# Column projections of the second stack's even layer as three rounded products, with the bias table loaded one phase later

## The reference, cut to what matters

```python
def even_mixer(hx, hc, w_in, gate_b, conv_w, conv_b, rpb, ml_norm_g, w_out, ctx_out):
    naq_x, nak_x, nav_x, mlqk_x, mlv_x, mlo_x, mlg_x = jnp.split(hx @ w_in, list(EVEN_SPLITS), axis=-1)
    naq_c, nak_c, nav_c, mlqk_c, mlv_c, mlo_c, mlg_c = jnp.split(hc @ w_in, list(EVEN_SPLITS), axis=-1)
    ...
    na_x = neighbourhood_attention(heads(naq_x), heads(nak_x), heads(nav_x),
                                   heads(nak_c), heads(nav_c), rpb)
    q_x, k_x, v_x, if_x, lf_x, ib_x, lb_x = _mlstm_inputs(mlqk_x, mlv_x, mlg_x + gate_b, conv_w, conv_b)
```

## Time and profile before

| | us |
|---|---|
| median of 3 runs | 3216.32 |
| lowest and highest of them | 3211.57, 3219.78 |
| the profiled execution | 3223.3 |
| its span in the trace | 3221.5 |
| TensorE busy | 2937.8 (91%) |
| VectorE busy | 1856.9 (58%) |
| ScalarE busy | 1409.2 (44%) |
| column projections, first to last product | 111.8 |

### The profile page before, as it was taken

How to read it: one execution, slowest core, us unless ns; L and a number is a source line. 1 busy time by engine, 2 the same in 40 slices (tenths; PEclk the granted TensorE clock), 3 DMA queues, 4 the chain that set the end, 5 groups by cost and what they waited for, 6 DMA issues and landing times. The chain is left out here.

```text
span 3221.5 us, 38728 instructions
## 1 busy us (share of the span) xinstructions
PE 2937.8 (91%) x15533; PEld 2270.3 (70%) x15533; DVE 1856.9 (58%) x2272; ACT 1409.2 (44%) x1799; POOL 13.5 (0%) x13
## 2 busy tenths in 40 slices
PE   6999899988799999999999989999779989799797
PEld 4799689777576676766766764448668767657796
DVE  3555454425688888888888830224444543345675
ACT  3221244324466676666666731223233333343554
POOL 0000000000000000000000000000000000000000
PEclk9999799999799999999999989899689999899898
DMA  4400364643799999989989973110012222201352
GB/s 158 144 1 1 138 228 171 262 144 132 275 361 345 351 342 346 347 339 345 350 334 352 359 277 94 62 53 4 14 61 92 92 92 79 78 35 40 120 182 79
DMA packets 94030, 585.86 MB, mean 182 GB/s; under 512 B 20400, under 2 KB 21504, under 8 KB 24480
## 3 DMA queue, kind: packets, MB, share of 16 engines
q1 hardware_dynamic: 91888, 580.26, 48.5%
q10 hardware_dynamic: 1968, 3.14, 0.3%
HBM read 582.31 MB, written 1.05 MB: 181 GB/s over the span
## 5 line engine op out<-in xcount | busy, mean ns | idle before, releaser
L2000 DVE TENSOR_TENSOR s_w_low<-weight_ring,s_w_high 128x2048 fp32r<-128x2048 f32 x336 | 759.7, 2289 | 127.0 <-ACT s_w_high L1939 123.2
L1939 ACT ACTIVATE s_w_high<-weight_ring 128x2048 fp32r<-128x2048 f32 x336 | 630.0, 1909 | 130.3 <-PE bank L1920 107.7
L254 DVE TENSOR_TENSOR s_w_low<-weight_ring,s_w_high 128x1024 fp32r<-128x1024 f32 x238 | 289.3, 1221 | 195.4 <-ACT s_w_high L239 195.2
L239 ACT ACTIVATE s_w_high<-weight_ring 128x1024 fp32r<-128x1024 f32 x238 | 249.5, 1051 | 282.9 <-PE bank L502 282.9
L502 PE MATMUL bank<-s_x_high,s_w_low 128*128 128x256 f32 (+1 forms) x1056 | 341.0, 323 | 28.9 <-DVE s_w_low L254 28.9
L1920 PE MATMUL bank<-s_w_high,s_x_low 128*96 128x512 f32 x896 | 356.4, 398 | 7.6 <-DVE s_w_low L2000 7.6
L1920 PE MATMUL bank<-s_w_high,s_x_high 128*96 128x512 f32 x896 | 356.8, 398 | 0.0
L1920 PE MATMUL bank<-s_w_low,s_x_high 128*96 128x512 f32 x896 | 354.4, 396 | 0.0
L502 PE MATMUL bank<-s_x_low,s_w_high 128*128 128x256 f32 (+1 forms) x1056 | 339.4, 321 | 0.0
L502 PE MATMUL bank<-s_x_high,s_w_high 128*128 128x256 f32 (+1 forms) x1056 | 339.2, 321 | 0.0
L356 PE MATMUL bank<-s_w_high,s_x_low 128*128 128x512 f32 x544 | 220.5, 405 | 59.8 <-DVE s_w_low L254 59.8
(11 more groups left out here) (468 smaller groups left out, 4164.8 us busy)
## 6 DMA issues: line engine op xcount, KB each, us to landing
weight_ring<-moe_w SPq DMA_DIRECT2D x336, 1024.0 KB, 6.7
weight_ring<-ada_w SPq DMA_DIRECT2D x48, 1024.0 KB, 6.1
weight_ring<-ffn_up SPq DMA_DIRECT2D x44, 1024.0 KB, 4.8
weight_ring<-ffn_w_in SPq DMA_DIRECT2D x22, 1024.0 KB, 4.9
weight_ring<-ffn_down SPq DMA_DIRECT2D x22, 1024.0 KB, 4.8
weight_ring<-ffn_w_down SPq DMA_DIRECT2D x11, 1024.0 KB, 4.8
weight_ring<-w_rkv_cols SPq DMA_DIRECT2D x8, 1024.0 KB, 8.3
weight_ring<-moba_qk SPq DMA_DIRECT2D x8, 1024.0 KB, 9.7
```

The lines of the kernel that those rows point to most:

```text
L239: K.nc.scalar.activation(self.hi[:, b, :], self.source(c, i), ACT.Copy).then_inc(*self.high.up())
L254: K.nc.vector.tensor_tensor(self.lo[:, b, :], self.source(c, i), self.hi[:, b, :], ALU.subtract)\
L1939: nc.scalar.activation(halves(whi, kind, n, i), raw(kind, n, i), ACT.Copy).then_inc(S["high"].h, 1)
L2000: V.tensor_tensor(halves(wlo, kind, n, i), raw(kind, n, i), halves(whi, kind, n, i), ALU.subtract)\
```

## The change

The function `linear_cols` is replaced, for this layer alone, by a new one, `split_cols`. It makes the parts of the 512 tokens once (ACT copies, DVE subtracts, four pieces of 128 x 1024 each), splits the weights by `Split` with depth 1, and issues three `fp32r` products where one in 32-bit floats stood: 384 of 128 x 128 by 128 x 512. The order of the outputs, the banks and the copies out are as before. The parts lie over units that nothing has filled yet: `x_high` over units 0 and 1, `w_high` over 2, `w_low` over 4, `x_low` over 7 and 8. Since `bias` is units 1 and 2, its 32 loads and that of `window` move from the column to the row projections, and the addition of `window` moves on DVE from the beginning of that phase to a place behind the running maximum, with a wait for the 33 loads ahead of it.

```diff
-    def __init__(self, K, st, chunks, depth, rows=None):
+    def __init__(self, K, st, chunks, depth, rows=None, bufs=None):
...
-        self.hi, self.lo = new("w_high", 2 * depth, CH // 2), new("w_low", 2 * depth, CH // 2)
+        self.hi, self.lo = bufs or (new("w_high", 2 * depth, CH // 2), new("w_low", 2 * depth, CH // 2))
...
+def split_cols(K, x, jobs, zero, parts_at, x_at):
...
+    chunks = sum(n for n, _ in jobs)
+    evac, zeroed, xsplit, xlow = K.sig(4)
+    parts = Split(K, None, chunks, 1, bufs=parts_at)
+    bank = lambda c, h: K.ps[c % 3 * 2 + h][:, :]
+    with K.begin() as block:
+        @block.tensor
+        def _(pe):
+            for c in range(chunks):
+                if c >= 3:
+                    pe.wait_ge(*evac.at(c - 2))
+                for i in range(2):
+                    pe.wait_ge(*parts.low.at(2 * c + i + 1))
+                    for h in range(2):
+                        for k in range(KT // 2):
+                            j = i * (KT // 2) + k
+                            if c == h == 0 and j % 2 == 0:
+                                pe.wait_ge(*xlow.at(j // 2 + 1))
+                            at = slice(k * 256 + h * P, k * 256 + h * P + P)
+                            for p, (ws, xs) in enumerate(((parts.lo, xhi), (parts.hi, xlo), (parts.hi, xhi))):
+                                last = nc.tensor.matmul(bank(c, h), ws[:, i, at], xs[:, j, :],
+                                                        start=(j == 0 and p == 0), stop=(j == KT - 1 and p == 2))
+                    last.then_inc(*(K.used if i else parts.half).up())
+                K.taken += 1
...
+        @block.gpsimd
+        def _(pool):
+            K.g(pool, nc.gpsimd.memset(zero, 0.0), zeroed)
...
+        @block.scalar
+        def _(act):
+            parts.act(act, -1)
+            for q in range(0, KT, 2):
+                nc.scalar.activation(xhi[:, q:q + 2, :], x[:, q:q + 2, :], ACT.Copy).then_inc(*xsplit.up())
+            act.wait_ge(*zeroed.at(1))
+            c = 0
+            for n, fn in jobs:
+                for m in range(n):
+                    parts.act(act, c)
+                    act.wait_ge(*K.used.at(c + 1))
+                    for h in range(2):
+                        last = fn(act, m, h, bank(c, h))
+                    K.a(act, last, evac)
+                    c += 1
...
+        @block.vector
+        def _(dve):
+            parts.dve(dve, -1)
+            for q in range(0, KT, 2):
+                dve.wait_ge(*xsplit.at(q // 2 + 1))
+                nc.vector.tensor_tensor(xlo[:, q:q + 2, :], x[:, q:q + 2, :], xhi[:, q:q + 2, :], ALU.subtract)\
+                    .then_inc(*xlow.up())
+            for c in range(chunks):
+                parts.dve(dve, c)
...
-        linear_cols(K, [(hT, 2, keep_apart(K, naq, 64 ** -0.5)), (hT, 2, keep(nak)), (hT, 4, keep(raw))],
-                    zero=naq[:, :, :])
+        over = lambda name, n, *shape: nc.alloc_sbuf_tensor_at(f"even_{name}", [P, *shape], F32R, offset=base + 4 * CH * n)
+        split_cols(K, hT, [(2, keep_apart(K, naq, 64 ** -0.5)), (2, keep(nak)), (4, keep(raw))], naq[:, :, :],
+                   (over("w_high", 2, 2, CH // 2), over("w_low", 4, 2, CH // 2)),
+                   (over("x_high", 0, KT, T2), over("x_low", 7, KT, T2)))
...
             K.v(dve, V.memset(peak[:, :, :], 0.0))
-            rows = bias.rearrange("p u (r c) -> p (u r) c", c=64)
-            K.v(dve, V.tensor_tensor(rows, rows, bc(window[:, :].unsqueeze(1), [P, 64, 64]), ALU.add))
...
             K.v(dve, last, peaked)
+            dve.wait_ge(*K.load.at(16 * 33))
+            rows = bias.rearrange("p u (r c) -> p (u r) c", c=64)
+            K.v(dve, V.tensor_tensor(rows, rows, bc(window[:, :].unsqueeze(1), [P, 64, 64]), ALU.add))
             dve.wait_ge(*peaks_back.at(1))
```

More of the change, by code:

```diff
@@ L309, in _ @@
                     late(dve, m)
+        @block.sync
+        def _(sp):
+            K.stream(sp)
+def split_cols(K, x, jobs, zero, parts_at, x_at):
+    nc = K.nc
+    xhi, xlo = x_at
+    chunks = sum(n for n, _ in jobs)
[48 more added lines that the diff above has]
+                parts.dve(dve, c)
@@ L2464, in even_layer @@
     with ExitStack() as st:
+        base = nc.sbuf_base
         units, = scratch(K, st, [P, 9, CH])
@@ L2474, in even_layer @@
         b5 = bias.rearrange("p (h q) (r c) -> p h q r c", q=TT, c=64)
+        raw, mlv, mlo = two(5), one(7), one(8)
+        cw, cb, gw, gb = scratch(K, inner, [P, KT, 3], [P, KT], [P, KT, 16], [P, 16])
+        tri, mask = scratch(K, inner, [P, 2, P], [P, 2, P])
+        K.later = [(cw[:, :, :], i["ev_conv_w"]), (cb[:, :], i["ev_conv_b"]), (gw[:, :, :], i["ev_w_gates"]),
+                    (gb[:, :], i["ev_gate_b"].partition_broadcast(P)), (tri[:, :, :], i["ml_tri"]),
+                    (mask[:, :, :], i["ml_mask"])]
+        keep = lambda dst, f=1.0: lambda act, c, h, o: nc.scalar.activation(dst[:, 2 * c + h, :], o, ACT.Copy, scale=f)
+        over = lambda name, n, *shape: nc.alloc_sbuf_tensor_at(f"even_{name}", [P, *shape], F32R, offset=base + 4 * CH * n)
+        split_cols(K, hT, [(2, keep_apart(K, naq, 64 ** -0.5)), (2, keep(nak)), (4, keep(raw))], naq[:, :, :],
+                   (over("w_high", 2, 2, CH // 2), over("w_low", 4, 2, CH // 2)),
+                   (over("x_high", 0, KT, T2), over("x_low", 7, KT, T2)))
         K.later = [(b5[64 * (qr % 2):64 * (qr % 2) + 64, h, qr // 2, :, :],
```

## The result

The changed kernel takes 3201.59 us, the median of 9 runs (3197.74 to 3206.15). The kernel before took 3218.21 in the same rounds (9 runs, 3211.47 to 3224.74). That is 16.6 us less; the ratio is 0.9944, with a 95% interval from 0.9932 to 0.9956. Run again later, in the rounds of one of the experiments, the changed kernel stood at 0.9942 (0.9922 to 0.9962). The prediction was 3198.7 us, in 3192 to 3206.5, and 17.6 us of gain.

A forecast was written before the change was run, and what follows sets the result against it. TensorE was taken to bound the kernel. The changed stage, start 4.6, slow products 5.1, others 84.1, last 0.39, gave 94.2 us against 111.8; 17.6 off the 3216.3 median gave 3198.7 us, range 3192 to 3206.5.

The forecast's parts named there:

- What bounds the stage: Column projections: TensorE alone bounds them, 111.8 us busy; what they lose the program loses, 17.6 us.
- The pace: Column projections: each rounded product takes 0.2267 us as in the FFN, three 0.680 against 0.858 for one 32-bit product.
- The rival with a quarter of L279's cost: Column projections: a product runs at 0.2145 us, saving 4.5 us more, 3194.2 us in all; chance 0.08.
- the sum: Column projections: 384 rounded products take 87.0 us against 109.8 for 128; whole stage 94.2 against 111.8, 17.6 shorter.
- the slow spell: Column projections' beginning: TensorE at half speed for 5.0 us, 12 products at 0.42; bounds 3.9 and 5.7 us.
- The start: Column projections' beginning: first product waits 4.60 us for DVE's first three steps; POOL's clear holding DVE would add 2.4.
- The sign named in the prediction: Column projections in the changed profile: TensorE waits for `w_low` once, 7.5 us at the start, and not again.
- The refill: Column projections' weight buffers: ready 2.3 to 2.4 us after release, needed after 5.44, so splitting costs nothing.
- Rivals 2 and 3: Column projections: TensorE waits 1.1 us at each of 16 halves (3216.3, chance 0.06), or refills are uncovered (3238, 0.03).
- Rival 3: Column projections: 14 halves refilled while TensorE stands, 2.4 us each plus 0.4 for restarts, 39 us: 3238; chance 0.03.
- The loads and DVE's addition: Row projections: 33 loads land in some 23 us, the 4.4 us addition fits 26.16 us of DVE idleness; cost nothing.
- The absolute time: Whole kernel: 3198.7 us, taken as the gain of 17.6 from the three earlier runs' median of 3216.3.

The follow-up runs named there:

- the other order: Changed kernel with ACT and DVE starting on first weight half, two token pieces, second weight half, two token pieces: stage 92.87 us against the changed kernel's 95.02.

## Why the prediction was right, point by point

- **What bounds the stage.** Right: 16.9 us less in a stage of TensorE alone is 16.6 us less in the medians and 18 by the ratio.
- **The pace.** Right: 0.2267 us a product was read from the FFN, and the removal of 128 products gives 0.2272. The rival with a quarter of L279's cost is out: at 0.2145 the stage would be 4.5 us shorter. The whole products under otherwise equal waits put the gain of this step at 22.3 us, where the sum had 22.8. The missing 0.5 is the slow spell, which cost 2.9 us in the changed kernel's execution and 2.4 in that of the whole products.
- **The start.** 4.76 us for 4.60. DVE's steps are as forecast: four token pieces take 4.63 us and one of them 1.22, so the first ends at 1922.96, 4.62 after the clear. TensorE starts 0.14 later. The sign named in the prediction was wrong in its name: the one wait at the start is for `x_low`, not for `w_low`. POOL's clear didn't hold DVE: its first subtraction starts 1.09 us after ACT's copy, and two take 2.36 us beside the clear, where they took 2.35 without. The Trainium skill, page "SBUF — State Buffer", section "SBUF: two separate sides", says that a DVE operation with two inputs is blocked only by a GpSimd operation that reads the memory. This trace agrees, with 2.36 us beside a clear of 3.52.
- **The slow spell.** The term that was sized worst: 5.0 us taken, 3.9 and 5.7 as bounds, 6.1 and 3.1 measured in two executions of the same kernel. Both bounds were single rows, and the length scatters by more than they lie apart. The lower one was read too long as well: in the kernel before, the granted clock is 1.00 from 1926.95 to 1927.5 and 0.50 only from there to 1930.9, 3.4 us. Against the forecast the spell was worth +0.6 us in the first profile and -0.9 in the second; the sum is right in spite of it, since it is small. That the gain of 16.9 us lies so near the forecast is in part luck, since the second profile of the same kernel has 18.3.
- **The refill.** Right that it costs nothing, as shown by the waits and by doubling DVE's work without effect. Rivals 2 and 3 are out. The FFN's nine waits in 252.5 us come every 28 us, not every 23 or 25 as the prediction has it; nothing hung on that. Rival 3's price was wrong, though it never had to be paid: the same mistake stands in the expectations for one product and for three more subtractions. A refill past the other half's time costs its excess once for each pair of buffers.
- **The loads and DVE's addition.** Right, both at nothing (0.9993 for them alone). The addition's old place gave nothing back and its new one has 21.7 us of idleness to spare.
- **The absolute time** is 2.9 us above the forecast: 1.9 of it is that the kernel before measured 3218.21 in the larger number of runs and not 3216.32, and 1.0 that the gain in the medians is 16.6 and not 17.6.

## What to carry to other kernels

When an operation is replaced by one that the kernel already uses in the same shape elsewhere, the price is in the trace, as the distance of starts and not as the row's duration, and here it was exact to a per cent. The cost of making its operands is then only the start, where nothing covers it, plus whatever exceeds the time that the other buffer covers; the latter is counted once for each round through the buffers. Before two profiles are compared, take milestones in untouched code: here a third of the difference of the spans lay ahead of the change.

## What the runs showed that I had not expected

A rounded product of 512 columns takes 0.227 us, a quarter of a whole one 0.2145; the factor is 0.79 for three against one, not 0.75. It is the same with one, two and three products on an operand, and with DVE busy or not. Why a rounded product costs 12 ns more was not tried and stays open.

The slow spell behind an idle stretch can be laid on products that nobody needs: ten fillers of 0.2 to 0.4 us in the 4.7 us of waiting left no real product slow, 2.9 us less than the changed kernel's first profile and 1.5 less than its second. That was one execution, and seven fillers with the other order left six slow, so how much of a spell they take isn't settled: TensorE had been idle for 2.9 us before the first filler in both, and the granted clock was 0.50 for 3.4 us in the one and 6.8 us in the other. What both are worth together at the median is below what 6 runs could tell.
